# Normalising attention queries after the scores instead of before them, in a two-block transformer kernel on one core

## What is computed

```
q = rms_norm(q.reshape(B, S, N_HEADS, HEAD_DIM), q_norm_g[l]).astype(jnp.float32) * HEAD_DIM ** -0.5
k = rms_norm(k.reshape(B, S, N_HEADS, HEAD_DIM), k_norm_g[l]).astype(jnp.float32)
...
scores = jnp.einsum('nbqhd,nbkhd->nbhqk', qb, kc)
scores = scores - slopes[:, None, None] * dist
scores = jnp.where(valid[None, :, None], scores, -jnp.inf)
m = jnp.max(scores, axis=-1, keepdims=True)
p = jnp.exp(scores - m)
```

## Time and profile before

| what | value |
|---|---|
| median of 3 runs (829.58 to 833.06) | 829.71 us |
| the profiled execution's own time | 830.8 us |
| its span, first to last instruction | 829.0 us |
| busy share: PE, PE weight loads, DVE, ACT, POOL | 99%, 92%, 78%, 67%, 28% |
| busy share of the 16 DMA engines, SP's queue | 55% |

### The profile page before, as it was taken

The page is one execution under the profiler, slowest core; times in us unless marked ns, Lnnn a source line. Parts: engine busy times, 40 slices in busy tenths (PEclk is TensorE's granted clock), DMA queues, the critical chain, the costliest instruction groups (busy, mean ns, idle before and its releaser), DMA issues.

```text
span 829.0 us, 16592 instructions
## 1 busy us (share of the span) xinstructions
PE 818.0 (99%) x6010; PEld 764.2 (92%) x6010; DVE 649.4 (78%) x1172; ACT 554.0 (67%) x1022; POOL 228.6 (28%) x245
## 2 busy tenths in 40 slices
PE   8999999999999999999999999999999999999996
PEld 8998998999999999999889989999998988888886
DVE  7998989997979998787766978756689866666552
ACT  8777999996756776666555776386647665655442
POOL 0387852332312244333101000020022333322110
PEclk9999999999999999999999999999999999999999
DMA  7666654546565376555646445435446566665741
GB/s 271 218 197 194 179 172 141 160 141 197 155 200 185 129 224 201 186 181 176 229 159 222 153 157 176 132 124 179 127 144 193 178 209 193 182 199 165 234 135 51
DMA packets 43168, 146.12 MB, mean 176 GB/s; under 512 B 4928, under 2 KB 7632, under 8 KB 43088
## 3 DMA queue, kind: packets, MB, share of 16 engines
q1 hardware_dynamic: 42192, 144.13, 55.0%
q10 hardware_dynamic: 896, 0.94, 0.4%
HBM read 144.00 MB, written 1.05 MB: 175 GB/s over the span
## 4 chain that ended last, share of the span: by engine, by line
PE 89%; DVE 5%; ACT 4%; issue 2%; DMA 1%; SPq 0%; DVEq 0%; ACTq 0%
PE px L561 20%; PE px L565 17%; PE px L567 16%; PE px L566 16%; PE px L562 10%; DVE wlo L1466 2%; PE px L571 1%; PE px L573 1%; PE px L572 1%; PE px L638 1%; PE px L787 1%; ACT whi L941 1%; DVE hx L1734 1%; PE px L650 1%; DMA raw<-ws 1%
## 5 line engine op out<-in xcount | busy, mean ns | idle before, releaser
L1466 DVE TENSOR_TENSOR wlo<-raw,whi 128x1024 fp32r<-128x1024 f32 x265 | 331.2, 1256 | 26.7 <-ACT whi L941 26.6
L941 ACT ACTIVATE whi<-raw 128x1024 fp32r<-128x1024 f32 x265 | 278.1, 1052 | 53.6 <-PE px L562 25.8
L565 PE MATMUL px<-hx,whi 128*128 128x256 f32 x1024 | 293.7, 287 | 0.9 <-DVE hx L1483 0.3
L566 PE MATMUL px<-hx,whi 128*128 128x256 f32 x1024 | 286.5, 280 | 0.0
L567 PE MATMUL px<-hx,wlo 128*128 128x256 f32 x1024 | 285.7, 279 | 0.0
L565 PEld LDWEIGHTS px<-hx,whi 128*128 128x128 f32 x1024 | 192.6, 188 | 4.5 <-issue 1.6
L566 PEld LDWEIGHTS px<-hx,whi 128*128 128x128 f32 x1024 | 192.9, 188 | 0.5
L567 PEld LDWEIGHTS px<-hx,wlo 128*128 128x128 f32 x1024 | 192.8, 188 | 0.0
L2119 POOL TENSOR_TENSOR CA<-CA,ct 128x256 f32<-128x256 f32 x90 | 89.9, 999 | 97.5 <-DVE wlo L1466 72.5
L561 PE MATMUL px<-fx,whi 128*128 128x512 f32 x330 | 114.5, 391 | 0.0
L561 PE MATMUL px<-hx,whi 128*128 128x512 f32 x320 | 111.1, 391 | 0.0
(11 more groups left out here) (331 smaller groups left out, 1319.1 us busy)
## 6 DMA issues: line engine op xcount, KB each, us to landing
raw<-ws SPq DMA_DIRECT2D x265, 512.0 KB, 3.6
tb<-tabs SPq DMA_DIRECT2D x16, 128.0 KB, 3.5
X<-xs SPq DMA_DIRECT2D x4, 256.0 KB, 4.0
raw<-ws SPq DMA_DIRECT2D x3, 256.0 KB, 5.7
out<-Y SPq DMA_DIRECT2D x1, 384.0 KB, 2.4
vc<-vecs SPq DMA_DIRECT2D x1, 315.5 KB, 7.0
raw<-ws ACTq DMA_DIRECT2D x1, 256.0 KB, 4.1
msk<-lmask ACTq DMA_DIRECT2D x1, 256.0 KB, 2.9
```

What stands on the lines that cost most here:

```text
L565: e.matmul(b[:, 0:S], H, xh, start=first, stop=False)
L566: e.matmul(b[:, 0:S], H, xl, start=False, stop=False)
L941: e.activation(whi[:, n % NSL, :], raw[:, n % NRAW, :], ACT.Copy).then_inc(s_hi, 1)
L1466: e.tensor_tensor(wlo[:, n % NSL, :], raw[:, n % NRAW, :], whi[:, n % NSL, :], ALU.subtract).then_inc(s_lo, 1)
```

## The change

Queries are no longer multiplied by 1 / rms. ACT's copy to `Q` multiplies by -1/8 times the gain. The score of a query row then is rms times too large, so DVE's custom operation takes 1 / rms of the row as its scale operand instead of 1.0, and the table, which is added ahead of the scaling, has to be multiplied by the rms first: GpSimd does so, in two instructions a head (`scaled_table`). For this the sums of the queries' squares are wanted with tokens in the partitions: two matmuls with the squares as the stationary operand and two columns of `bd` as the moving one write four columns (two halves of the tokens, two heads) beside the keys' sums in the same PSUM bank. One Ln and one Exp over 260 columns, and an Exp of 4 columns for the rms itself, serve a pair of jobs (`head_rms`). The tables grow from 256 to 384 columns, since the second part's columns now need another factor than the first's, and 10 KB a partition of new buffers (`hn`, `qm`, the wider `tb`, and a filler of 256 bytes) stand ahead of the later ones.

```diff
-            tb = sb(c, "tb", [P, 3, S])
+            tb = sb(c, "tb", [P, 3, 384])
+            hn = sb(c, "hn", [P, KD, S + 4])
+            qm = sb(c, "qm", [P, KD, 4])
+            gap(c, "gap5", 256)
...
+        def query_norm(of, h, half):
+            n = 2 * half + h % 2
+            return of[:, h // 2, n:n + 1]
+        hq = hn[:, :, S:S + 4]
...
             def head_sums(m):
-                b = take(("hs", m), SMALL if m < 8 else VALUES if m < 15 else FEW)
                 e.wait_ge(s_hsq, m + 1)
                 e.wait_ge(s_con, 5)
+                if m % 2 == 0:
+                    b = take(("hs", m // 2), SMALL if m < 8 else VALUES if m < 14 else FEW)
+                    e.matmul(b[:, S:S + 2], hsq[:, m % 3, tokens(0)], bd[:, 0:P:64], start=True, stop=True,
+                             skip_group_check=True)
+                    e.matmul(b[:, S + 2:S + 4], hsq[:, m % 3, tokens(1)], bd[:, 0:P:64], start=True, stop=True,
+                             skip_group_check=True).then_inc(s_hsum, 1)
+                    return
+                b = px_of["hs", m // 2]
                 e.matmul(b[:, 0:S], bd[:, :], hsq[:, m % 3, :], start=True, stop=True).then_inc(s_hsum, 1)
...
+            def head_rms(i):
+                M = rst[:, i % 2, 0:S + 4]
+                e.wait_ge(s_hsum, 2 * i + 2)
...
+                e.activation(M, px_of["hs", i][:, 0:S + 4], ACT.Ln, bias=vec("eps"), scale=1.0 / 64).then_inc(
+                    BANK["hs", i][0], 1)
+                e.wait_ge(*BANK["hs", i])
+                e.activation(hn[:, i, :], M, ACT.Exp, scale=-0.5).then_inc(s_hr, 1)
+                e.activation(qm[:, i, :], M[:, S:S + 4], ACT.Exp, scale=0.5).then_inc(s_qm, 1)
...
-                e.tensor_tensor_reduce(sS_[:, j, 0:S], b[:, 0:S], T, 1.0, 3e38, ALU.add, ALU.min, mx_[:, h, 2:3])
-                e.tensor_tensor_reduce(sS_[:, j, S:384], b[:, S:384], T[:, P:S], 1.0, 3e38, ALU.add, ALU.min,
+                e.tensor_tensor_reduce(sS_[:, j, 0:S], b[:, 0:S], T[0], scales[0], 3e38, ALU.add, ALU.min, mx_[:, h, 2:3])
+                e.tensor_tensor_reduce(sS_[:, j, S:384], b[:, S:384], T[1], scales[1], 3e38, ALU.add, ALU.min,
...
+            def scaled_table(h):
+                T = tb[:, h % 3, :]
+                e.wait_ge(s_tb[h % 3], 16 * (h // 3 + 1))
+                e.wait_ge(s_qm, h // 2 + 1)
+                e.tensor_scalar(T[:, 0:S], T[:, 0:S], query_norm(qm, h, 1), None, ALU.mult)
+                e.tensor_scalar(T[:, S:384], T[:, S:384], query_norm(qm, h, 0), None, ALU.mult).then_inc(s_ts, 1)
+
+            table_at = {FILL1[n][0] - 1: (n, n + 1) for n in range(0, NH, 2)}
             for m in range(len(QKG)):
+                for h in table_at.get(m, ()):
+                    scaled_table(h)
                 qkg(m)
```

More of the change, by code:

```diff
@@ L432, in two_blocks @@
         s_hsq, s_hsum, s_hr, s_hsc = sem("s_hsq"), sem("s_hsum"), sem("s_hr"), sem("s_hsc")
+        s_qm, s_ts = sem("s_qm"), sem("s_ts")
         s_sc, s_exp, s_rec, s_nrm, s_tr, s_pv, s_ohi = (
@@ L681, in _ @@
                 if n < NH and n % 2 == 0:
-                    e.wait_ge(s_hsc, n + 2)
+                    e.wait_ge(*BANK[("q", n // 2), 0])
+                    e.wait_ge(s_hsc, n // 2 + 1)
                     if n == 0:
@@ L1090, in qkg @@
                 if 0 <= m - 2 < 16:
[L1091 to L1098, removed]
+                    if m % 2:
+                        head_rms((m - 3) // 2)
                 if (w, i) == ("g", 1):
@@ L1106, in qkg @@
                     e.activation(hsq[:, m % 3, :], px_of[(w, i), 0][:, 0:S], ACT.Square).then_inc(s_hsq, 1)
-                    e.activation((Q if w == "q" else K)[:, i, :], px_of[(w, i), 0][:, 0:S], ACT.Copy).then_inc(
-                        BANK[(w, i), 0][0], 1)
+                    if w == "q":
+                        e.wait_ge(s_cst, 4)
+                        e.activation(Q[:, i, :], px_of[(w, i), 0][:, 0:S], ACT.Copy, scale=qg8[:, 0:1]).then_inc(
+                            BANK[(w, i), 0][0], 1)
+                    else:
+                        e.activation(K[:, i, :], px_of[(w, i), 0][:, 0:S], ACT.Copy).then_inc(BANK[(w, i), 0][0], 1)
                 elif i:
@@ L1281, in _ @@
             e.dma_start(wg2[64:80, :], w_gate2).then_inc(s_wg2, 16)
-            e.dma_start(caus[:, :], tabs[NH]).then_inc(s_caus, 16)
+            e.dma_start(caus[:, :], tabs[NH][:, 0:S]).then_inc(s_caus, 16)
             e.dma_start(msk[:, :], masks).then_inc(s_msk, 16)
@@ L2055, in _ @@
                 if 0 <= n - 1 < MH:
-                    softmax(1, n - 1, caus[:, :], sS2, mx2)
+                    softmax(1, n - 1, (caus[:, :], caus[:, P:S]), sS2, mx2)
                 if 0 <= n - 3 < MH:
@@ L2276, in shape_constants @@
     lc = np.where(count > 0, np.log(np.maximum(count, 1)), NEG)
-    tabs = np.empty((NH + 1, P, S), np.float32)
+    tabs = np.empty((NH + 1, P, 384), np.float32)
     for h in range(NH):
         slope = 2.0 ** (-8.0 * (h + 1) / NH)
-        tabs[h] = -np.where(count > 0, lc - slope * d, NEG)
-    tabs[NH] = -np.where(d >= 0, 0.0, NEG)
+        tabs[h, :, 0:S] = -np.where(count > 0, lc - slope * d, NEG)
+    tabs[NH, :, 0:S] = -np.where(d >= 0, 0.0, NEG)
+    tabs[:, :, S:384] = tabs[:, :, P:S]
     j, i = np.arange(P)[:, None], np.arange(P)[None, :]
```

25 lines of the change are left out of this document (11 added, 14 removed).

## The result

| | before | after |
|---|---|---|
| median | 829.48 us (828.85 to 833.06, 10 runs) | 832.73 us (832.15 to 833.93, 10 runs) |
| profiled execution, its span | 830.8, 829.0 us | 832.84, 831.0 us |

The medians lie 3.25 us apart. The ratio of the runs is 1.0035, 95% interval 1.0026 to 1.0044: the change costs a little over a third of a percent. The profiled execution of before lies 1.3 us above its median, that of after at its median, so the two spans differ by only 2.0 us.

The account below looks back on a forecast made before the run. PE was taken as the bound, 89% of the chain, with one 0.8 us wait on ACT. +0.1 (PE) and -0.7 (ACT) made -0.6 against the profiled 830.8: 830.2, forecast as median 829.1 us; range 827.2 to 831.6.

Parts of the forecast that it names:

- PE, +0.1: PE's sums: four passes at 0.11 us replace one 0.43 us sum, +0.1 us over 8 pairs; steps stay 3.24 us.
- Rival A: On PE, weight loads hide and the sums become cheap: up to 3.4 us more gained, 825.7 us; chance 0.08.
- ACT, -0.7: Fewer Ln and Exp let ACT's copy come some 0.7 us earlier; PE's 0.8 us wait near 143 falls to 0.1.
- GpSimd's price: Table instructions: 0.5 to 0.74 us for 256 columns, some 0.29 to 0.45 for 128; 13 to 19 us for 16 heads.
- The margin in step 9: POOL's taps behind the first tables are done by about 115, ACT wants the first about 115.5: some 1 us margin.
- rival C: Late tables hold ACT if GpSimd takes over 1.2 us for 256 columns: 829.8 to 830.8 us; chance 0.12.
- spare time up to 126: Even if POOL's taps of step 9 came late, ACT has spare time before 126 us to absorb the miss.
- Later tables come two steps ahead: Tables after the first come two steps ahead of their use, so neither DVE's softmax nor ACT is held.
- DVE, "nothing, as long as the lead covers it": Scale operands add 1.8 us on DVE, 1.2 of it after step 17, against 4.0 us lead: no cost at the end.
- the weight ring's 4.0 us: Late in the stage DVE's remainder `wlo` of a weight chunk is ready 4.0 us before PE comes to it.
- Rival B: GpSimd and DVE block each other, DVE becomes the bound: PE waits 4.6 us near 200, 833.7 us; chance 0.12.
- the rule named with rival B: A two-SBUF-input DVE instruction and a GpSimd one reading SBUF exclude each other throughout: 11.8 us on DVE, 838.

Follow-up runs that it names:

- no_pass_const_scale: The changed kernel without GpSimd's table pass and with constant 1.0 as the custom operation's scale, so scores are wrong: 828.58 us, 0.9989.
- early_first_tables: The changed kernel with the first three tables issued three chunks earlier and the first two scaled at POOL's step 7, nothing left out: 831.90 us, 1.0028.
- the square: Four variants of the changed kernel: light taps with early first tables 828.97 us, full taps with early 831.90, light with late 829.89, full with late 832.73.
- light_taps: The changed kernel with two of DVE's taps a chunk on 16 columns from step 14 on, part of the convolution left out: 829.89 us, 1.0007.
- before_vector_scale: The kernel before with the custom operation's scale read from a column of ones instead of the constant 1.0: 830.35 us, 1.0012.
- paced_tables: early_first_tables with one head's table pass a step, each behind the wait for DVE's split and ahead of the taps: 835.92 us, 1.0074.

## Why the prediction was wrong

The forecast was 829.1 us and the range ended at 831.6; the time is 832.73. That it would be within 0.5% of before held; the sign of the small difference did not. (The interval of the ratio is 0.18% wide, so 0.5% was also too much for what a measurement can tell.)

- **PE, +0.1: held.** A pass of two columns costs its 128-column weight load; steps stay at 3.24 us. Rival A is out.
- **ACT, -0.7: the mechanism held, the place didn't.** Ln over 260 columns lasts 476 ns, Exp 422, the small Exp 190 and the copy to `Q` 472 against 375 for `K`, all as priced. In no_pass_const_scale the wait near 143 is gone and the time is 0.8 us better, against the 0.6 forecast. In the kernel itself it is lost again to the first tables, see below.
- **GpSimd's price: mis-sized.** Undisturbed, 0.93 us for 256 columns and 0.61 for 128, where the bounds were 0.5 to 0.74 and 0.29 to 0.45. The upper bound, that one input costs no more than a tap's two, had nothing behind it but the two rows, and was passed. A head costs 1.53 us undisturbed, and the 32 instructions last 29.2 us in all where 13 to 19 were forecast.
- **The margin in step 9 held, and one pair later there was none (rival C, in part).** The first tables are done at 113.1, DVE starts the second head at 113.12, not 111.63, and the taps behind them end at 115.6, for which ACT doesn't wait. It waits behind the second pair's tables, which the prediction didn't look at:

```profile
121.54 1.89 POOL L2174 TENSOR_SCALAR tb<-tb,qm 128x256 f32<-128x256 f32 x1
...
125.53 1.81 POOL L2145 TENSOR_TENSOR CA<-CA,ct 128x256 f32<-128x256 f32 x1
...
127.37 0.91 ACT L1059 ACTIVATE ct<-CI,cw 128x256 f32<-128x256 f32 x2 [1.69 <-POOL CA L2145]
```

The prediction gave ACT spare time up to 126; this wait begins at 125.7. Both of GpSimd's instructions are stretched as well (1.89 and 1.81 us in the place of 0.93 and 0.74). PE's wait near 143 is then 0.9 us in the place of 0.1. In early_first_tables, where everything of GpSimd's before that lies earlier, the same tap is done at 124.5 and the wait is gone; that run and the square put 0.8 to 0.9 us on it. Rival C had said 829.8 to 830.8, and light_taps, with this and no other loss, has 829.89; but its trigger, over 1.2 us for 256 columns, wasn't met.

- **"Later tables come two steps ahead": false.** A table's slot is free only after DVE's pass over head h - 3, so POOL waited for later tables' DMA 3.7 us in 3 waits (1.86 at 158.37), with the taps queued behind it.
- **DVE, "nothing, as long as the lead covers it": the step that failed.** The price was right, 0.055 a custom operation. The lead was the wrong one (and before_vector_scale, with the operand alone, costs 1.0 us). I held DVE's extra time against the weight ring's 4.0 us, which was never touched. DVE hands PE three other things in a step: normalised probabilities, an empty score bank, and the low part of the values. Of these the bank had 1.0 to 1.5 us, and the row that shows DVE at 11.89 of 12 while PE never waits was a warning: an engine that is full for over forty microseconds has no slack to give, only a lead to spend. Account: before, DVE loses 0.1 to 0.3 us a pair; the scale operand adds 0.2 and the stretching 0.5.
- **Rival B: the right side, with the wrong trigger.** GpSimd and DVE do hold each other up, and DVE becomes the bound. It was to decide from 2.8 us of collisions against 4.0 of lead; 2.1 us more than before, with the operand's 0.2 a pair, was enough against a bank lead of 1.0. It counted splits as the victims and table instructions as the culprits. The normalisation (1.3 us) suffered more than the splits (0.9), and the culprits are often POOL's own old taps, pushed out of a place where they met nothing that minds them. I had noted that the taps were kept behind the split, but not that a pass ahead of them would move them off it.

On the rule named with rival B, the Trainium skill's page "SBUF — State Buffer" (Who interferes with whom): it also says that a DVE instruction with at most one SBUF input doesn't contend outside certain fast modes, and that `tensor_scalar` can enter them. The traces agree in both halves: taps with one SBUF input 479 ns beside a table instruction and 479 elsewhere, the normalisation up to 0.76 us in the place of 0.28 (0.78 in the place of 0.35 in paced_tables). What I had made of it, that each meeting costs DVE a whole GpSimd instruction (11.8 us in all, 838), does not hold: the stretching between 144 and 184 us is 2.6 us, and no single DVE instruction was stretched by much over 0.5 us.

What stays open: how much of the 2.9 us (what the full taps cost in the square) is the stretching and how much the scale operand can't be split cleanly, since both draw on one lead. Alone on no_pass_const_scale the operand costs 1.4 us (829.96) and the pass 3.25 (831.83); together they cost 4.15 and not 4.6. A pass that never meets the normalisation wasn't found, so a run without any stretching but with the pass's late tables and waits doesn't exist.

## What to carry to other kernels

When an engine is full but nobody waits for it, list everything that it hands over in a step, PSUM banks it empties among them, and take the shortest lead, by name, from the timelines; compare its time for one period of the loop with that of the engine that it feeds, because a lead is spent once and a rate is paid every period. An instruction put ahead of others in an idle engine's queue costs through what it pushes: look where the pushed instructions land, and which instructions of another engine they stretch there. For an instruction with no row in the trace, a bound "no worse than one with more inputs" is not a bound.

## Not expected of the hardware

- GpSimd's multiplication of [128, 256] float32 by one value a partition lasts 927 ns, longer than its addition of two such tiles (742); [128, 128] lasts 607.
- A value a partition in the place of a constant costs DVE's custom operation 55 ns at both widths (419 to 474, 286 to 341), and ACT's copy from PSUM 97 ns (375 to 472).
- DVE's multiplication in place in SBUF by one value a partition (353 and 280 ns) is stretched by GpSimd's work to 0.78 and 0.76 us, as the two-input split is, from 1.22 to 1.43 or more; a multiply-add with one input in SBUF and one in PSUM is not (479 ns either way). GpSimd's own instruction can be the one that is held: 1.52 us in the place of 0.61 over a split of 1.21.
- Float32 matmuls with 2 moving columns and new weights of 128 columns cost 0.11 us a pass at the full clock, a quarter of a 256-column sum of 0.43 us.
